# A hybrid RG-LRU, Fourier and mixture-of-experts layer on one core: the Fourier branch folded by symmetry, four gates, the gelu and one modulation moved

## The chip, the cores and the metric

One Trainium2 chip, one of its cores. The metric is the time of one execution on the device in microseconds (us), as the median of the runs. The engines are TensorE (PE; its weight loads are the rows PEld), VectorE (DVE), ScalarE (ACT), GpSimd (POOL), and SyncE (SP), which issues most DMAs.

## What is computed

384 tokens of 1024 channels: 128 context tokens and 256 latent ones, which share all weights. All matrix products are in fp32. Cut to what matters:

```python
def trunk_layer(x, mod, h0, p):
    sh1, sc1, g1, sh2, sc2, g2 = [mod[:, k, None, :] for k in range(6)]   # mod = silu(cond) @ w_ada + b_ada
    u = (x * (1.0 + sc1) + sh1) @ p['w_in']           # 1536 columns: xr, gr, xf, 512 each
    xr = centred_conv(xr, ...)
    yr, states = rglru_bidir(xr, ...)                 # gates, then one scan per direction, summed
    yr = yr * jax.nn.gelu(gr)
    yf = fourier_mix(xf, p['fn_w'], p['fn_b'])
    mix = jnp.concatenate([yr, yf], axis=-1) @ p['w_out']
    x = layer_norm(ALPHA * x + g1 * mix, ...)
    y2 = hier_moe(x * (1.0 + sc2) + sh2, ...)         # top expert group, two of its four experts of 1024x512
    return layer_norm(ALPHA * x + g2 * y2, ...), states

def fourier_mix(x, w, b):                             # 4 groups of 128 channels
    f = jnp.fft.fft2(xg, axes=(positions, channels), norm='ortho').real
    return einsum('bngi,gij->bngj', f, w) + b
```

## The kernel before, in words

The kernel is one program of five instruction streams that meet at semaphores; the order on each engine is written out by hand. Tokens lie along the free dimension for the mixer, in tiles of 388 columns (W: 128 context, 3 of padding, 256 latent, 1), and channels on the partitions.

**Weights.** SP streams 17 units of 2 MB (`p1_units`: twelve of `w_ada`, three of `w_in`, two of `w_out`) and then 48 expert units (`order`) through a ring of six, later seven, slots (L368, L387). A unit's load waits until `p1_used` or `unit_used` says that the slot's last reader is done. Expert units 3, 4 and 5 wait for `p1_used` 15, 16 and 17 (17 is the second G2 sum), unit 6 for the first LayerNorm's results.

**Modulation.** For each of twelve halves n, `ada_sums(n)` (PE, L1284, 32 columns wide) forms partial sums in a PSUM bank (ABANK), ACT copies them to the one buffer `mrow` (`ada_rows`, L446), `ada_cols(n)` (PE, L1295) turns them into columns, and DVE adds the bias (`mod_out`, L772). Halves 4 to 9 come between the mixer's branches and the output projection, 10 and 11 (second gate, G2) after it, ahead of the routing.

**Mixer.** PE computes twelve tiles of the input projection (`project(w)`, L1346: w 0 to 3 are xr, 4 to 7 xf, 8 to 11 gr) and places eight gate products among them (`gate(it)`, L1329) as GATE_WITHIN and GATE_AFTER say: 0 to 3 by tiles 4 to 6, 4 and 5 by tile 7, 6 and 7 by tile 8. ACT makes four activations of each (L480 to L488), POOL two operations (L1219, L1220), DVE two (L822, L823); after gates 3 and 7 ACT takes one square root over four gates (L491, with a table load), and DVE runs scans and sums (L828 to L848). gelu: POOL makes its argument and last product (L1229 to L1234), ACT the tanh (L495).

**Fourier branch.** For each channel group g: `chan_dft` (L1365) multiplies three token tiles by the channel DFT, 256 columns each; ACT copies the result to Z (L522, L523); `pos_dft` (L1376, L1380) multiplies by the position DFTs, two products of 128 columns and four of 256, into bank 4; DVE copies to FTs (L857); `fourier_out` (L1388) applies `fn_w` into bank 5; DVE adds the bias (L859). The groups lie one behind the other behind tiles 8 to 11, and share one bank each for result and output.

**Output projection and routing.** L1447 forms the mix in 48 products of 512 columns, with broadcasts of modulation rows between them (`row`, L1431); it begins once all of `ada_cols` to 9, `yf_sb` and `yr_done` are there. DVE makes LayerNorm and the second modulation (L904 to L917). Then PE: `ada_sums(10)`, `ada_cols(10)`, `h2_cols(0)` (eight transposes, L1460), `ada_sums(11)`, `ada_cols(11)`, `h2_cols(1)`, `logits(0)`, `logits(1)` (L1466), `h2_cols(2)`, `logits(2)`. DVE chooses the experts (L927 to L965), PE ranks the tokens (L1490, L1495), DVE builds selection matrices (L984, L994), and PE gathers each expert's tokens (`dispatch`, L1509). The sixteen experts follow (L1547, L1553, L1585, L1592, L1620), and a second LayerNorm.

## Time and profile before

| | us |
|---|---|
| median of three runs | 546.44 |
| the three runs | 542.8, 546.44, 548.4 |
| span of the profiled execution, first to last instruction | 544.4 |
| mean of the granted TensorE clock in it, as a share of full speed | 0.936 |

The profiled execution has no time of its own beside its span; the span is 2.0 us under the median of the runs. In the rows, an instruction group has its start, its duration, engine, line, operation, output<-input with shapes, and how often it occurs; in square brackets stands the engine's idle time before it and what ended that. An fp32 product is two MATMUL instructions in the rows.

### The profile page before, as it was taken

The page shows a single profiled execution, that of the slowest core. Times are in us where ns is not written, and L with a number is a line of the kernel's source. Part 1 is how long each engine was busy: PE and PEld are TensorE (multiplying, and loading weights), DVE is VectorE, ACT ScalarE, POOL GpSimd, SP SyncE. Part 2 cuts the span into 40 slices and gives each one's busy share as a digit, 9 for nine tenths or more (in the row PEclk, how much of TensorE's full clock was granted, in tenths as well). Part 3 has the DMA queues.
Part 4 walks back from the last instruction along what each step waited for, and adds up shares of the span by engine and source line. Part 5 has one row for each costly group of instructions (what it writes and reads, how often), then busy time and mean ns, then how long its engine had stood idle before and what let it go on. Part 6 is the DMA issues. An engine that isn't in the chain of part 4 may idle for free.

```text
span 544.4 us, 6675 instructions
## 1 busy us (share of the span) xinstructions
PE 465.0 (85%) x2488; PEld 261.0 (48%) x2488; DVE 244.5 (45%) x440; ACT 120.6 (22%) x224; POOL 61.4 (11%) x59
## 2 busy tenths in 40 slices
PE   0788997979899999839799999999999999899600
PEld 0444554647455653739645545455555554454200
DVE  2552626580314319565011324444444444334797
ACT  2300177841210220313401111111111111021100
POOL 1000042673400006610000000000000000000000
PEclk9989999998999999858999999999999999999855
DMA  8999692200999405950059999999999999999002
GB/s 321 387 386 291 244 390 68 96 1 18 308 389 387 169 1 184 391 198 2 1 195 389 390 392 340 396 395 393 391 393 394 395 395 393 392 391 377 11 2 116
DMA packets 64868, 146.64 MB, mean 269 GB/s; under 512 B 3560, under 2 KB 4392, under 8 KB 64824
## 3 DMA queue, kind: packets, MB, share of 16 engines
q1 hardware_dynamic: 63776, 143.66, 71.4%
q10 hardware_dynamic: 888, 2.28, 1.1%
q8 instruction: 30, 0.49, 0.4%
q0 software_dynamic: 160, 0.10, 0.3%
q14 instruction: 14, 0.11, 0.1%
HBM read 144.45 MB, written 1.58 MB: 268 GB/s over the span
## 4 chain that ended last, share of the span: by engine, by line
PE 73%; DVE 12%; DMA 5%; issue 5%; ACT 4%; ACTq 0%; SPq 0%; DVEq 0%
PE PS L1547 16%; PE PS L1346 9%; PE PS L1585 8%; PE PS L1447 8%; PE PS L1553 5%; PE PS L1284 4%; PE PS L1620 4%; DMA ring<-in_ex_w_gate 4%; PE PS L1509 4%; PE PS L1431 2%; PE PS L1295 2%; PE PS L1329 2%; PE PS L1466 2%; PE PS L1592 1%; PE PS L1627 1%
## 5 line engine op out<-in xcount | busy, mean ns | idle before, releaser
L1547 PE MATMUL PS<-ring,xs 128*64 128x256 f32 x896 | 103.1, 382 | 1.8 <-DMA ring<-in_ex_w_gate 1.1
L1547 PEld LDWEIGHTS PS<-ring,xs 128*64 128x64 f32 x896 | 62.4, 137 | 37.9 <-issue 9.7
L1346 PE MATMUL PS<-hT,ring 128*128 128x388 f32 x192 | 68.3, 510 | 3.8 <-DVE hT L793 3.8
L1585 PE MATMUL PS<-ring,hTs 128*64 128x512 f32 x224 | 52.7, 613 | 1.3 <-DMA ring<-in_ex_w_down 0.8
L1098 DVE SCALAR_TENSOR_TENSOR y<-PS,comb,y 128x1024 f32<-128x1024 f32 x42 | 53.5, 1277 | 0.3 <-PE PS L1627 0.3
L1346 PEld LDWEIGHTS PS<-hT,ring 128*128 128x128 f32 x192 | 37.8, 198 | 31.4 <-issue 5.2
L1553 PE MATMUL PS<-ring,xs 128*128 128x512 f32 x64 | 28.1, 594 | 2.9 <-ACT xs L611 2.9
L1585 PEld LDWEIGHTS PS<-ring,hTs 128*64 128x64 f32 x224 | 15.2, 140 | 31.4 <-issue 31.3
L645 ACT CAST yh<-PS 128x512 fp32r<-128x512 f32 x14 | 8.2, 586 | 97.9 <-PE PS L1585 58.1
L1084 DVE TENSOR_TENSOR yl<-PS,yh 128x512 fp32r<-128x512 f32 x14 | 9.7, 692 | 43.9 <-ACT yh L645 43.9
L1620 PE MATMUL PS<-yh,selT 64*128 64x512 f32 x84 | 21.0, 496 | 4.6 <-DVE y L1098 2.6
L1284 PE MATMUL PS<-ring,cond 128*32 128x512 f32 x192 | 23.4, 611 | 0.0
L1447 PE MATMUL PS<-ring,yfs 128*128 128x512 f32 x48 | 23.4, 633 | 0.0
L1054 DVE SCALAR_TENSOR_TENSOR hid<-sg,PS 128x256 f32<-128x256 f32 x14 | 5.9, 422 | 38.7 <-PE PS L1547 38.7
L1447 PE MATMUL PS<-ring,mixT 128*128 128x512 f32 x48 | 21.6, 592 | 0.0
L1620 PEld LDWEIGHTS PS<-yh,selT 64*128 64x128 f32 x84 | 8.0, 186 | 26.2 <-issue 26.1
L1553 PEld LDWEIGHTS PS<-ring,xs 128*128 128x128 f32 x64 | 12.0, 190 | 17.2 <-issue 17.1
L1509 PE MATMUL PS<-sel,h2H 128*128 128x384 f32 x48 | 17.9, 373 | 2.6 <-DVE sel L994 2.6
L1219 POOL TENSOR_SCALAR gtmp<-gtmp 128x388 f32<-128x388 f32 x8 | 9.5, 1188 | 85.9 <-ACT gtmp L481 85.9
L1295 PEld LDWEIGHTS PS<-cst,mrow 128*128 128x128 f32 x96 | 11.7, 191 | 13.1 <-ACT mrow L446 7.3
L446 ACT COPY mrow<-PS 128x512 f32<-128x512 f32 x12 | 7.0, 586 | 46.8 <-PE PS L1284 37.9
L1509 PE MATMUL PS<-sel,h2L 128*128 128x384 f32 x48 | 17.3, 360 | 0.0
(230 smaller groups left out, 601.3 us busy)
## 6 DMA issues: line engine op xcount, KB each, us to landing
ring<-in_ex_w_gate SPq DMA_DIRECT2D x16, 2048.0 KB, 13.8
ring<-in_ex_w_up SPq DMA_DIRECT2D x16, 2048.0 KB, 14.0
ring<-in_ex_w_down SPq DMA_DIRECT2D x16, 2048.0 KB, 14.5
ring<-in_w_ada SPq DMA_DIRECT2D x12, 2048.0 KB, 14.8
ring<-in_w_in SPq DMA_DIRECT2D x3, 2048.0 KB, 20.6
ring<-in_w_out SPq DMA_DIRECT2D x2, 2048.0 KB, 12.4
xn<-in_x_sample SPq DMA_DIRECT2D x2, 512.0 KB, 6.5
pos<-in_pos SPq DMA_DIRECT2D x2, 512.0 KB, 7.5
```

The lines of the kernel that those rows point to most:

```text
L1098: dve.scalar_tensor_tensor(out=y12[:, i, :], in0=src, scalar=comb[:, i, e:e + 1], in1=y12[:, i, :], op0=ALU.mult, op1=ALU.add).then_inc(s[ ...
L1284: mm = pe.matmul(PS[32 * j:32 * j + 32, ABANK[n], :], cond32[:, k, :], w[:, k, :], start=(k < 4), stop=(k >= 4))
L1295: mm = pe.matmul(PS[:, 7, 2 * (c0 + q):2 * (c0 + q) + 2], mrow[:, q * P:(q + 1) * P], cst[:, C_SUM:C_SUM + 2], start=True, stop=True)
L1329: mm = pe.matmul(PS[:, 4 + gi, 0:W], wbd[:, 8 * gi + 4 * d + c, :], xc[:, c, :], start=True, stop=True)
L1346: mm = pe.matmul(PS[:, w % 4, 0:W], wt[:, k, (w % 4) * P:(w % 4 + 1) * P], hT[:, k, :], start=(k == 0), stop=(k == KD - 1))
L1431: mm = pe.matmul(PS[:, 6 + k // 4, (k % 4) * P:(k % 4 + 1) * P], modT[:, j * KD + k, q:q + 1].broadcast_to([P, P]), ident, start=True, sto ...
L1447: mm = pe.matmul(PS[:, 2 * i + h, :], x, unit3(ring[(14 + h) % RING])[:, c, :], start=(n == 0), stop=(n == KD - 1))
L1509: mm = pe.matmul(PS[:, 4 + n % 4, 0:HS], part[:, i, k * P:(k + 1) * P], sel[:, i, h * HS:(h + 1) * HS], start=(i == 0 and part is h2H), st ...
L1547: mm = pe.matmul(PS[HALF * h:HALF * (h + 1), j, 0:FE // 2], x[:, k, 0:HALF], w[:, k, h * (FE // 2):(h + 1) * (FE // 2)], start=(k == 0), s ...
L1553: mm = pe.matmul(PS[:, j, :], x[:, k, :], w[:, k, :], start=(k == 0), stop=(k == KD - 1))
L1585: mm = pe.matmul(PS[HALF * h:HALF * (h + 1), 3, :], x, w[:, f, h * 512:(h + 1) * 512], start=(f == 0), stop=(f == KF - 1))
L1620: mm = pe.matmul(PS[:, b + h, :], m[HALF * h:HALF * (h + 1), i * P:(i + 1) * P], part[HALF * h:HALF * (h + 1), 0:512], start=(q == 0), sto ...
```

## The change

The Fourier branch uses symmetry and reordering. `fn_w` is multiplied into the channel DFT beforehand on chip (`chan_maps`: two products of 512 columns, copied by ACT to `maps`), and the position DFT is folded: DVE adds and subtracts mirrored positions (`folds`), so that the cosine part needs one half of the rows and the sine part the other. `chan_dft` then makes six products of 128 columns per group (two of them with 64 output rows on each half), `pos_dft` one of 128 and two of 256 columns into bank g, and its result is the output up to the bias. `FTs` and the old `fourier_out` on PE are gone. All four groups come after tile 11; `ada_sums` 4 and 5 stand between them and use banks 5 and 4.

Gates 4 to 7 move behind tiles 9, 10 and 11. The square roots become `mult(0)` (after tile 6) and `mult(1)` (after tile 11, ahead of the Z copies). The gelu's argument moves from POOL to DVE among the gates, its tanh becomes one ACT operation of 1552 columns after `ada_rows(4)`, its last product a DVE operation. `mod_out` 4 and 5 stand after two of the four gelu products. The Fourier bias is added by DVE after each scan of the second half.

After the output projection `ada_sums` 10 and 11 and `ada_cols(10)` come after `logits(2)`, `ada_cols(11)` after the ranking; ACT's and DVE's parts move with them (DVE's `mod_out` 10 and 11 behind the ranking's sums).

```diff
-        GATE_WITHIN = {5: 1, 6: 3, 7: 4, 8: 6}
-        GATE_AFTER = {4: 0, 5: 2, 7: 5, 8: 7}
+        GATE_WITHIN = {5: 1, 6: 3, 10: 5, 11: 7}
+        GATE_AFTER = {4: 0, 5: 2, 9: 4, 10: 6}
...
-        ABANK = [6, 6, 4, 6] + [6, 4] * 3 + [6, 6]
+        ABANK = [6, 6, 4, 6] + [5, 4] * 3 + [6, 6]
...
+                if w == 6:
+                    mult(0)
+                if w == 8:
+                    act.wait_ge(s["maps_ps"], 1)
+                    act.copy(maps[:, :, :], PS[:, 6:8, :]).then_inc(s["maps_sb"], 1)
+
+            def z_copy(g):
+                act.wait_ge(s["z_ps"], g + 1)
+                if g >= 2:
+                    act.wait_ge(s["f_ps"], g - 1)
+                act.copy(Z[:, g % 2, :], PS[:, 6 + g % 2, 0:TOK]).then_inc(s["z_sb"], 1)
+
+            mult(1)
+            for g in range(FG):
+                z_copy(g)
...
-            for n in range(4, 10):
+            ada_rows(4)
+            act.wait_ge(s["gelu_t"], CR)
+            act.activation(xf[:, :, :], xf[:, :, :], ACT.Tanh, scale=float(np.sqrt(2 / np.pi))).then_inc(s["gelu_th"], 1)
+            for n in range(5, 10):
                 ada_rows(n)
...
             root(NT + 1)
+            h2_copies(0)
+            h2_copies(1)
+            root(NT + 2)
+            h2_high(0)
+            h2_high(1)
+            h2_copies(2)
             ada_rows(10)
-            h2_high(0)
-            h2_copies(0)
-            root(NT + 2)
+            h2_high(2)
             ada_rows(11)
-            h2_high(1)
-            h2_copies(1)
-            h2_copies(2)
-            h2_high(2)
...
+            def folds():
+                dve.wait_ge(s["win_sb"], 8)
+                dve.wait_ge(s["conv_done"], CR)
+                dve.wait_ge(s["zeroed"], 4)
+                for n, (c0, m) in enumerate(SEG):
+                    o, h = (0, P)[n], m // 2
+                    a_, b_ = xf[:, :, c0 + 1:c0 + h], xf[:, :, c0 + m - 1:c0 + h:-1]
+                    step(dve.tensor_tensor(fold[:, :, o + 1:o + h], a_, b_, ALU.add))
+                    step(dve.tensor_tensor(fold[:, :, o + h + 1:o + m], a_, b_, ALU.subtract))
+                    step(dve.tensor_copy(fold[:, :, o:o + 1], xf[:, :, c0:c0 + 1]))
+                    step(dve.tensor_copy(nyq[:, :, n * HALF:n * HALF + 1], xf[:, :, c0 + h:c0 + h + 1]))
+                    step(dve.memset(fold[:, :, o + h:o + h + 1], 0.0))
...
+            def gelu_arg(c):
+                t_, g = xf[:, c, :], gr[:, c, :]
+                dve.wait_ge(s["win_sb"], 8 + c + 1)
+                link(dve.tensor_tensor(t_, g, g, ALU.mult))
+                link(dve.tensor_scalar(t_, t_, 0.044715, 1.0, ALU.mult, ALU.add))
+                dve.tensor_tensor(t_, t_, g, ALU.mult).then_inc(s["gelu_t"], 1)
...
             for b in range(2):
+                if b:
+                    folds()
+                    gelu_arg(0)
+                    gelu_arg(1)
...
+                    if it >= 6:
+                        gelu_arg(it - 4)
...
+                    if b:
+                        fourier_out(it - 4)
...
+            dve.wait_ge(s["gelu_th"], 1)
             for c in range(CR):
-                dve.wait_ge(s["gelu_done"], c + 1)
+                link(dve.scalar_tensor_tensor(out=gr[:, c, :], in0=xf[:, c, :], scalar=1.0, in1=gr[:, c, :],
+                                              op0=ALU.add, op1=ALU.mult))
...
+                if c == 1:
+                    mod_out(4)
+                    mod_out(5)
-            for n in range(4, 10):
+            for n in range(6, 10):
                 mod_out(n)
...
+            def chan_maps():
...
+                for h in range(2):
+                    mm = pe.matmul(PS[:, 6 + h, :], dft[:, F_CH + h * P:F_CH + (h + 1) * P],
+                                   fnw[:, :, :].rearrange("p g n -> p (g n)"), start=True, stop=True)
+                mm.then_inc(s["maps_ps"], 1)
...
             def chan_dft(g):
...
+                pe.matmul(PS[0:HALF, b, 0:P], fold[:, g, 0:HALF], co, start=True, stop=True)
+                pe.matmul(PS[HALF:P, b, 0:P], fold[:, g, HALF:P], si, start=True, stop=False)
+                pe.matmul(PS[HALF:P, b, 0:P], nyq[:, g, 0:HALF], co, start=False, stop=True)
+                pe.matmul(PS[:, b, P:2 * P], fold[:, g, P:2 * P], co, start=True, stop=True)
+                pe.matmul(PS[:, b, 2 * P:3 * P], fold[:, g, 2 * P:3 * P], si, start=True, stop=False)
+                pe.matmul(PS[:, b, 2 * P:3 * P], nyq[:, g, HALF:], co, start=False, stop=True).then_inc(s["z_ps"], 1)
 
             def pos_dft(g):
...
+                pe.matmul(PS[:, g, 0:SEQ], z[:, 0:P], dft[:, F_CTX:F_CTX + P], start=True, stop=True)
                 for m in range(2):
...
+                    mm = pe.matmul(PS[:, g, SEQ:TOK], z[:, (1 + m) * P:(2 + m) * P],
+                                   dft[:, F_LAT + LAT * m:F_LAT + LAT * (m + 1)], start=(m == 0), stop=(m == 1))
                 mm.then_inc(s["f_ps"], 1)
...
+                if w == 7:
+                    chan_maps()
+
+            pe.wait_ge(s["win_sb"], 12)
+            pe.wait_ge(s["gate_act"], 8)
+            chan_dft(0)
+            chan_dft(1)
             ada_sums(4, 7)
+            ada_sums(5, 8)
+            for g in range(FG):
+                pos_dft(g)
+                if g + 2 < FG:
+                    chan_dft(g + 2)
             ada_cols(4)
...
             pe.wait_ge(s["row_sb"], 6)
-            ada_sums(10, 15)
-            ada_cols(10)
             h2_cols(0)
-            ada_sums(11, 16)
-            ada_cols(11)
             h2_cols(1)
...
             pe.transpose(PS[0:8, 2, 128:256], stin[:, 0:8], ident).then_inc(s["st_ps"], 1)
+            ada_sums(10, 15)
+            ada_sums(11, 16)
+            ada_cols(10)
...
             mm.then_inc(s["rank_ps"], 1)
+            ada_cols(11)
```

## Rows read from the trace of the kernel before

**Rows 1.** The page's head, and the DMA engines' busy tenths in 40 slices.
```profile
span 544.4 us, 6675 instructions
DMA  8999692200999405950059999999999999999002
```

**Rows 2.** Groups by line and form on PE, 87.41 to 161.09 us: busy, mean ns, idle before.
```profile
L1284 PE MATMUL PS<-ring,cond 128*32 128x512 f32 x96 | 11.3, 597 | 0.0
L1380 PE MATMUL PS<-dft,Z 128*128 128x256 f32 x32 | 8.6, 416 | 0.0
L1365 PE MATMUL PS<-dft,xf 128*128 128x256 f32 x24 | 6.6, 415 | 0.0
L1295 PE MATMUL PS<-cst,mrow 128*128 128x2 f32 x48 | 6.3, 253 | 0.7 <-ACT mrow L446 0.7
L1329 PE MATMUL PS<-xc,wbd 128*128 128x388 f32 x16 | 5.9, 494 | 2.8 <-ACT gtmp L481 2.8
L1388 PE MATMUL PS<-FTs,fnw 128*128 128x384 f32 x8 | 3.4, 512 | 0.2 <-DVE FTs L857 0.2
L1376 PE MATMUL PS<-dft,Z 128*128 128x128 f32 x16 | 2.7, 290 | 4.6 <-DVE FTs L857 3.9 <-ACT Z L523 0.7
```

**Rows 3.** Windows: length, busy (x) of PE, PEld, DVE, ACT, POOL, then granted clock.
```profile
87.41:161.09 73.68, 65.37 (x314) 39.66 (x313) 32.47 (x60) 29.22 (x50) 30.53 (x32) 0.98 0.44 149
...
226.00:244.81 18.81, 8.90 (x60) 8.14 (x60) 8.66 (x38) 3.55 (x5) 6.08 (x5) 0.50 0.69 255
244.81:265.80 20.99, 20.94 (x108) 19.73 (x108) 8.34 (x35) 7.92 (x17) 0.00 (x0) 0.88 0.00 1
```

**Rows 4.** PE in order of time: products of known size.
```profile
103.44 1.46 PE L1365 MATMUL PS<-dft,xf 128*128 128x256 f32 x6
104.73 5.38 PE L1346 MATMUL PS<-hT,ring 128*128 128x388 f32 x16
...
166.17 3.60 PE L1447 MATMUL PS<-ring,mixT 128*128 128x512 f32 x8
...
173.04 1.95 PE L1431 MATMUL PS<-cst,modT 128*128 128x128 f32 x16
```

**Rows 5.** ACT in order of time: two gates' first activations, a table load, a square root.
```profile
92.89 0.58 ACT L480 ACTIVATE rtmp<-PS,bga 128x388 f32<-128x388 f32 x1
...
96.12 0.59 ACT L480 ACTIVATE rtmp<-PS,bga 128x388 f32<-128x388 f32 x1
...
106.62 1.28 ACT L491 ACT_TABLE_LOAD   x1
108.56 1.50 ACT L491 ACTIVATE gtmp<-gtmp 128x1552 f32<-128x1552 f32 x1 [0.65 <-DVE gtmp L823]
```

**Rows 6.** Groups by line and form on DVE, 90 to 160 us.
```profile
L848 DVE TENSOR_TENSOR xc<-hfb 128x256 f32<-128x256 f32 x4 | 2.7, 682 | 0.1
```

**Rows 7.** Groups by line and form on PE, 214.82 to 244.81 us.
```profile
L1284 PE MATMUL PS<-ring,cond 128*32 128x512 f32 x32 | 3.8, 598 | 0.0
L1295 PE MATMUL PS<-cst,mrow 128*128 128x2 f32 x16 | 2.1, 252 | 1.5 <-ACT mrow L446 1.5
```

**Rows 8.** PE in order of time, the last transposes and logits.
```profile
228.42 1.95 PE L1460 MATMUL PS<-cst,tts 128*128 128x128 f32 x8
231.47 3.61 PE L1466 MATMUL PS<-wr,h2T 128*128 128x20 f32 x16 [1.10 <-ACT h2T L547]
```

**Rows 9.** DVE in order of time: the last h2, the routing's first and last steps.
```profile
221.55 1.28 DVE L914 SCALAR_TENSOR_TENSOR tts<-tts,stat,rows 128x1024 f32<-128x1024 f32 x1
...
235.11 0.22 DVE L927 TENSOR_TENSOR lg<-PS,rb 128x60 f32<-128x60 f32 x1 [9.14 <-PE PS L1466]
...
241.12 0.21 DVE L965 TENSOR_TENSOR before<-rt 128x48 bf16<-128x48 f32 x1
```

**Rows 10.** The chain that ended last, in order of time: start, us, what.
```profile
161.09 12.10 PE PS L1447 x24
...
451.47 19.65 DMA ring<-in_ex_w_gate
```

More of the change, by code:

```diff
@@ L216, in build @@
         xf = at("xf", o, [P, FG, W]); o += FG * W * 4
-        Z = at("Z", o, [P, 2, NT, 2 * P]); o += 2 * NT * 2 * P * 4
+        Z = at("Z", o, [P, 2, TOK]); o += 2 * TOK * 4
         dft = at("dft", o, [P, NDFT]); o += NDFT * 4
+        maps = at("maps", o, [P, 2, FG * P]); o += 2 * FG * P * 4
         fnw = at("fnw", o, [P, FG, P]); o += FG * P * 4
         hfb = at("hfb", o, [P, 2, W]); o += 2 * W * 4
+        nyq = at("nyq", o, [P, FG, HALF + P]); o += FG * (HALF + P) * 4
         assert o <= end
@@ L488, in gate, with mult @@
                 act.activation(tr, a_, ACT.Square).then_inc(s["sq_done"], 1)
-                if q == 3:
-                    act.wait_ge(s["rec_v"], it + 1)
-                    act.activation(gtmp[:, 2], gtmp[:, 2], ACT.Sqrt, scale=-1.0).then_inc(s["mult_done"], 1)
-            def gelu_tanh(c):
-                act.wait_ge(s["gelu_t"], c + 1)
-                act.activation(xpad[:, c, 0:W], xpad[:, c, 0:W], ACT.Tanh, scale=float(np.sqrt(2 / np.pi)))\
-                    .then_inc(s["gelu_th"], 1)
+            def mult(b):
+                act.wait_ge(s["rec_v"], 4 * b + 4)
+                act.activation(gtmp[:, 2], gtmp[:, 2], ACT.Sqrt, scale=-1.0).then_inc(s["mult_done"], 1)
             for w in range(12):
@@ L516, in _ @@
                     gate(GATE_AFTER[w])
-                if w >= 8:
-                    act.wait_ge(s["z_ps"], c + 1)
-                    if c >= 2:
-                        act.wait_ge(s["f_ps"], c - 1)
-                    act.copy(Z[:, c % 2, 0:2, :], PS[:, 6, :].rearrange("p (i n) -> p i n", n=256))
-                    act.copy(Z[:, c % 2, 2, :], PS[:, 7, 0:256]).then_inc(s["z_sb"], 1)
-                    gelu_tanh(c)
+                if w == 6:
[11 more added lines that the diff above has]
+                z_copy(g)
             for r, n in enumerate(("ln_in_g", "ln_in_b")):
@@ L918, in _ @@
                     .then_inc(s["x1n"], 1)
-            for n in range(10, 12):
-                mod_out(n)
             low_part(0)
@@ L978, in _ @@
             dve.nop().then_inc(s["pw_done"], 1)
+            for n in range(10, 12):
+                mod_out(n)
             def pick(m):
@@ L1353, in chan_dft @@
             def chan_dft(g):
-                pe.wait_ge(s["win_sb"], 4 + g + 1)
                 if g == 0:
-                    pe.wait_ge(s["smallw_in"], 32)
-                    pe.wait_ge(s["mod_sb"], 4)
-                    pe.wait_ge(s["mrow_sb"], 4)
-                else:
-                    pe.wait_ge(s["z_sb"], g)
-                for i in range(NT):
-                    out = PS[:, 6, i * 256:(i + 1) * 256] if i < 2 else PS[:, 7, 0:256]
-                    mm = pe.matmul(out, xf[:, g, TC[i]:TC[i] + P], dft[:, F_CH:F_CH + 256], start=True, stop=True)
@@ L1366, in chan_dft @@
-                mm.then_inc(s["z_ps"], 1)
+                    pe.wait_ge(s["maps_sb"], 1)
+                    pe.wait_ge(s["fold_done"], 1)
+                if g >= 2:
+                    pe.wait_ge(s["z_sb"], g - 1)
+                b = 6 + g % 2
+                co, si = (maps[:, h, g * P:(g + 1) * P] for h in range(2))
+                pe.matmul(PS[0:HALF, b, 0:P], fold[:, g, 0:HALF], co, start=True, stop=True)
+                pe.matmul(PS[HALF:P, b, 0:P], fold[:, g, HALF:P], si, start=True, stop=False)
```

72 lines of the change are left out of this document (19 added, 53 removed).

## The prediction, made before the changed kernel was run

> **What bounds the kernel now.** I read the page first: a span of 544.4 us, 2.0 under the median of the runs, and a DMA row that is at 9 from slice 20 to slice 36 [rows 1], so the experts' weights stream without a pause from about 275 us on. The chain of waits then puts PE at nearly every step up to there, and only late, at 451.47 us, a piece of 19.65 us on an expert load [rows 10]. The stream of expert units beyond the seven that are preloaded starts when the first expert product ends. Whether PE or the stream ends last among the experts, both hang on the moment at which the experts start. So what is won or lost ahead of them passes to the end one for one, and I take the experts and the final LayerNorm as unchanged.
>
> Ahead of them are two stretches in which PE isn't filled. From 87.41 us (gate 4) to 161.09 us (start of the output projection) PE is busy 65.37 of 73.68 us [rows 3], so it idles 8.3 us. The groups name 8.3 of it: 2.8 ahead of the gates, 4.6 and 0.2 in the Fourier branch, 0.7 ahead of the last `ada_cols` [rows 2]. From the end of the projection, which I call E (214.82 us), to the dispatch at 244.81 us [rows 3], PE works through small products and then waits for DVE's routing; the clock is at the low level, 0.50, from 226.00 us on and stays there for some 5 us of dispatch (0.88 over 20.99 us is 5.0 us at half) [rows 3].
>
> **Stretch 1, what goes.** The old Fourier products are L1380, L1365, L1388 and L1376: 8.6 + 6.6 + 3.4 + 2.7 = 21.3 us [rows 2]. A printed group runs about 0.17 us into its successor (1.46 us, but the next starts after 1.29 [rows 4]); for 16 such groups that is 2.7, so 18.6 us of PE's time go.
>
> **What comes.** `chan_maps`: two products of 512 columns. Eight instructions of that size take 3.60 - 0.17 = 3.43 us [rows 4], 0.43 each, so four take 1.7. `chan_dft`: six products of 128 columns, twelve instructions; sixteen take 1.78 [rows 4], 0.111 each, so 1.33 per group and 5.3 for four. The trace before has no fp32 product with 64 output rows at this size. If the two halves ran side by side a group would take 1.1, and if each product cost as much as one of 256 columns (0.43) it would take 2.6: 4.4 to 10.4 us, and I take 5.3, as 128 columns are the row nearest. `pos_dft`: 0.22 + 2 x 0.43 = 1.08, four are 4.3. Sum 11.3. PE's work falls by 18.6 - 11.3 = 7.3 us.
>
> A rule of the Trainium skill speaks against the new `chan_dft`: TensorEngine Tiling (Array Packing), Key Properties, says that a change between tiling modes drains TensorE. The L1284 products are 32 wide and alternate with 128-wide ones, and their groups have 0.0 us of idle before them over 96 instructions [rows 2]; by the rule eight more switches would cost something, by the row nothing that can be seen, and I take nothing.
>
> **Laying out the new order on PE.** After gate 3 there is no Fourier work and no gate until tile 9. From 87.4 us: 4.5 tiles at 5.21 (16 instructions, 5.38 - 0.17 [rows 4]) are 23.4, four gates (5.9 - 4 x 0.17) 5.2, the maps 1.7: tile 11 ends at about 117.7. ACT needs 3.23 us per gate with a copy (96.12 - 92.89 [rows 5]) where PE gives it one each 3.9, so it keeps up: gate 4 from 103.6, with a table load of 1.28 [rows 5], gate 7 done at 118.1, last copy 118.6. `chan_dft` 0 and 1: to 121.4. Sums 4 and 5 are 2 x 1.8 (11.3 us for six, less overlaps [rows 2]): to 125.0. They cover `mult(1)`: DVE's last reciprocal parts end at 119.5, table load and square root (1.28 + 1.50 [rows 5]) at 121.4, the Z copies by 122.4. This cover is 2.6 us; without it PE would wait that long. The rest of the Fourier work, 7.0: to 132. Then four sums (7.2) and six `ada_cols` (6.3 less overlaps, 5.9), with 1.4 us of waits for ACT: the tanh over 1552 columns (by the square root 1.50, plus a load of 1.28) stands ahead of `ada_rows(5)` and costs 0.5 of it. The projection starts at 146.6 instead of 161.09, 14.5 earlier. The other account, 7.3 of work and 8.3 - 2.3 of idle, gives 13.3. I take 14.0.
>
> Beside the path: `folds` handles 1520 elements per partition and six tiny ones. At 682 ns for 256 [rows 6] that is 4.0 us, at half that rate 2.0; it lies between DVE's last scan of the first half (about 97.5) and gate 4's results (107.9), with `gelu_arg(0)`, as tile 9's copy (102.7) holds `gelu_arg(1)` back anyway. Its cover is about 5 us; beyond that it delays gates 6 and 7 by the recurrence's waits, one for one. Three gelu operations of 388 elements are at most 3.1 us per tile by the same row, hidden while ACT paces DVE. DVE's Fourier bias waits for `f_ps` between scans, where the next scan is queued behind it; this ends by 134.5. The tanh ends at 134.5, four times 1.45 us of products end at 140.3, and the projection asks for them first at 146.6: 6 us of cover. `mod_out` 4 and 5, which `ada_cols(6)` waits for, come at 137.4, just in time. POOL loses 20 operations, none on the path. On SP's queue the loads of `w_out` wait for sums 4 and 5, which move from 143 and 148 to 123 and 125 us, 20 us before use. No stall here.
>
> **Stretch 2.** The two sums and `ada_cols` pairs leave PE's path ahead of the transposes: L1284 with 3.8 us, L1295 with 2.1 and 1.5 of waits [rows 7]. `h2_cols(0)`, `(1)` and `logits(0)`, `(1)` then end by about E + 6. What is late next is DVE's third h2, ready at 222.83, E + 8.0 [rows 9]; `h2_cols(2)` ran at 228.42, E + 13.6 [rows 8]. It moves 5.6 us ahead. From there to DVE's first routing step are 6.7 us at the low clock [rows 8, 9]; I keep them, since only transposes and products of 20 columns then stand between E and the logits, and the clock fell before in just such work. Logits at E + 14.7. DVE's selection takes 6.2 (235.11 to 241.33 [rows 9]): E + 20.9. PE's moved work must fit beneath it: the state's transpose 0.4, sum 10 at the low clock 3.8 (2 x 1.9 [rows 7]), ACT's copy 0.6, sum 11. Dispatch brought the clock back after 5 us of dense work; by that it is back at E + 20.2, sum 11 ends at E + 21.8, `ada_cols(10)` at E + 22.8: ranking starts 1.9 late. From there to the dispatch 3.5 as before (241.33 to 244.81), plus 0.3 for the two `mod_out` that now stand ahead of the selection matrices: E + 26.6 instead of E + 30.0, a gain of 3.4. Dispatch begins at the full clock: 2.5 of its 5 slow us were not spent waiting for DVE's matrices, and half of that is 1.2. Sum 4.6.
>
> Expert units 4 to 6 wait behind the moved sums: unit 6 is loaded by about E + 40 at 5.3 us each and is read some 90 us after E. Nothing waits.
>
> **Sum.** 14.0 + 4.6 = 18.6 us: span 525.8, and on the median 546.4 - 18.6 = **527.8 us**.
>
> **The rivals.**
> *The clock is full through the routing.* The last logits end at E + 11.9, the sums lie beneath the selection (E + 18.1), dispatch at E + 21.9: 8.1 + 1.2, 23.3 in all: 523.1 us. For it: sums are dense and now come late. Against: the 11 us behind E are thinner than before.
> *The clock stays low until dispatch.* Then sum 11 ends at E + 23.3, `ada_cols(10)` at E + 25.3, and `ada_cols(11)` takes 2.0 ahead of DVE's `mod_out`: dispatch at E + 29.9, no gain in stretch 2, 14.1 in all: 532.3 us. For it: the low level held through 226.00 to 244.81 [rows 3]. The Trainium skill, TensorE: Matmul & The Clock Gate, Part 4, says that transposes do not count as PE being busy, which makes an earlier fall likely; the trace agrees in so far as the fall came among transposes and logits.
> *The tail of the second gates bounds PE.* The idle of 8.3 us stays, now as waits for Z, tanh or `mod_out`: 12.6 in all, 533.8 us. For it: `mod_out` has no slack and ACT has a table load on each side. Against: sums 4 and 5 fill the largest gap.
> *Slower: the folds.* Reversed rows of a three-dimensional tile are in no row before. From 5 us on they delay the gates; from 5 + 18.6 = 23.6 us on (15.5 ns per element, six times the row) the kernel is slower. At 30 us it would be 552.8.
> *Nothing arrives*, because the experts' end does not follow their start: 546. Against: [rows 1].
>
> **How the numbers follow.** Forecast 0.42, full clock 0.17, low clock 0.21, tail 0.14, folds 0.03, nothing 0.03. One per cent is about what a measurement of this kernel can tell from no change. Faster by over 1% (under 541) 0.94, within 1% 0.03, slower 0.03. The runs before lie 3.6 below to 2.0 above their median; I take the full clock less 3 as the low end, the tail plus 3 as the high end: 520 to 537, which leaves out some 0.15 with what scatters. The dear `chan_dft` (5.1 more) ends at 532.9, inside.
>
> **What would show it.** In the profile after: tile 11 ends near 118 us, the first L1447 product near 147, and PE's idle from gate 4 on is 2 to 3 us; the new `chan_dft` takes 1.3 us a group; the folds 2 to 4 us in all. The third transposes start 8.0 us after E, DVE's routing at E + 14.7, dispatch at E + 26.6; the clock is low from about E + 5 to E + 20. The experts take as long as before from dispatch to end. It is wrong if a wait over 2 us stands ahead of `pos_dft`, `ada_cols` or the first mix product, or if experts wait longer for weights.

## The result, and the profile after

The changed kernel takes 531.41 us, median of 4 runs (530.14 to 532.37), beside 547.42 us (542.8 to 551.39, 4 runs) for the kernel before on the same chip: 16.0 us less. The run of 551.39, 1.6% above the fastest, counts as a slow one: without it the kernel before has 546.44 and the gain is 15.0 us, and the ratio, 0.9739 with the interval 0.9691 to 0.9787, goes by fast runs alone. The forecast was 527.8 (520 to 537). The profiled execution has a span of 528.9 us, 15.5 under the span of before [rows 1], where the sum had promised 18.6. So the question is less whether there is a gain than where the missing 3 us went.

I cut both kernels at the same moments, read from PE in order of time, so that each stretch has a length of its own. E is taken here less the 0.17 that a group runs into its successor, 214.65 for the kernel before where the prediction says 214.82.

```
                                      before    after   change   forecast
start to the first projection           31.07    33.36    +2.3      0
first projection to gate 3              49.82    49.57    -0.25     0
gate 3 to the first mix product         80.07    66.06   -14.0    -14.0
first mix product to E                  53.69    53.70     0        0
E to the dispatch                       30.16    25.59    -4.6     -3.4
dispatch, first to last product         20.95    21.48    +0.5     -1.2
last dispatch to first expert product    2.92     2.93     0        0
first expert product to the end        275.72   276.21    +0.5      0
span                                   544.4    528.9    -15.5    -18.6
```

**Stretch 1** (gate 3 to the first mix product) came out to a tenth. PE's groups by line and form, kernel after, 92.06 (the maps) to 148.99 us (first mix product), beside [rows 2]:

```profile
L1315 PE MATMUL PS<-ring,cond 128*32 128x512 f32 x96 | 11.3, 597 | 0.0
L1326 PE MATMUL PS<-cst,mrow 128*128 128x2 f32 x48 | 6.2, 252 | 1.0 <-ACT mrow L448 1.0
L1360 PE MATMUL PS<-xc,wbd 128*128 128x388 f32 x16 | 5.9, 489 | 0.0
...
L1403 PE MATMUL PS<-maps,fold 128*64 128x128 f32 x8 | 1.7, 298 | 0.8 <-ACT gr L512 0.8
```

The waits of 2.8 ahead of the gates and of 4.6 and 0.2 in the Fourier branch [rows 2] are gone; left are 1.0 for ACT's row copies and 0.8 for its copy `gr`. The windows from gate 3 on give the split. A row has the length, then PE's, PEld's, DVE's, ACT's and POOL's busy time, then the granted clock:

```profile
80.89:160.96 80.07, 71.76 (x334) 43.33 (x332) 35.15 (x64) 34.53 (x58) 33.78 (x36) 0.98 0.42 142
```

is the kernel before, and

```profile
82.93:148.99 66.06, 64.20 (x330) 37.63 (x328) 39.32 (x86) 33.51 (x51) 15.26 (x16) 1.00 0.54 184
```

is the kernel after. PE's busy time falls by 71.76 - 64.20 = 7.6 and its idle from 8.3 to 1.9, by 6.4. Not all of the 7.6 is work that went. In the kernel before, a wait for DVE's `FTs` was followed by the low level of the clock (PE in order of time):

```profile
122.42 0.68 PE L1376 MATMUL PS<-dft,Z 128*128 128x128 f32 x4 [2.61 <-DVE FTs L857]
122.94 2.90 PE L1380 MATMUL PS<-dft,Z 128*128 128x256 f32 x8
125.63 2.18 PE L1365 MATMUL PS<-dft,xf 128*128 128x256 f32 x6
```

The same two groups take 1.89 and 1.46 elsewhere (133.95 and 135.68), so 1.7 us of the old busy time came from the clock. The stretch's granted clock was 0.98 before and is 1.00 now. For the kernel after, PE in order of time shows what a channel group of the new `chan_dft` costs:

```profile
120.82 0.32 PE L1403 MATMUL PS<-maps,fold 128*64 128x128 f32 x1 [0.81 <-ACT gr L512]
120.82 0.32 PE L1404 MATMUL PS<-maps,fold 128*64 128x128 f32 x1
...
121.95 0.39 PE L1408 MATMUL PS<-maps,nyq 128*128 128x128 f32 x2
122.27 0.32 PE L1403 MATMUL PS<-maps,fold 128*64 128x128 f32 x1
...
123.72 3.64 PE L1315 MATMUL PS<-ring,cond 128*32 128x512 f32 x32
127.29 0.49 PE L1414 MATMUL PS<-dft,Z 128*128 128x128 f32 x2
127.62 1.03 PE L1416 MATMUL PS<-dft,Z 128*128 128x256 f32 x4
...
129.71 0.39 PE L1408 MATMUL PS<-maps,nyq 128*128 128x128 f32 x2
129.94 0.39 PE L1414 MATMUL PS<-dft,Z 128*128 128x128 f32 x2
```

From one group to the next are 122.27 - 120.82 = 1.45 us (forecast 1.33). The two halves with 64 output rows start at the same moment. The Trainium skill, TensorEngine Tiling (Array Packing), Key Properties, says that tiles can run in parallel, and the trace agrees. With the halves side by side the forecast's own prices give 1.1 for a group, so the measured 1.45 is 0.35 above them, and not only 0.12. Part of that lies where the width changes: L1408 takes 0.32 us up to the next product where that is 64 wide (121.95 to 122.27), and 0.23 where it is 128 wide (129.71 to 129.94). `ada_cols` shows the same 0.09, with 1.05 behind a 32-wide sum (140.62, no wait) and 0.96 behind a 128-wide product (134.65). The same section says that a change of mode drains TensorE; the trace agrees in so far as each change goes with some 0.1 us, which stands inside the busy time and not in the idle column. A group has two changes; the rest of the 0.35 stays open.

Sums 4 and 5 cover the square root of `mult(1)` in full: no wait stands at 127.29. On DVE the reversed fold of 508 elements per partition costs 1.34 ns per element, half of what I had taken:

```profile
99.72 0.68 DVE L833 TENSOR_TENSOR fold<-xf 128x508 f32<-128x508 f32 x1
...
102.32 0.56 DVE L847 TENSOR_TENSOR xf<-xf,gr 128x388 f32<-128x388 f32 x1
```

The second row, a product that reads forwards, costs 1.44 ns per element, so reading backwards costs nothing that can be seen here. The row that I had priced by, L848, is a poor measure: its eight instructions before took 280 to 941 ns, for a reason that stays open.

The whole of `folds` is 2.4 us, from 98.90 to 101.3 (forecast 4.0, low bound 2.0).

**Stretch 2** (E to the end of the dispatch), PE in order of time, kernel after. E is 202.69:

```profile
204.92 4.87 PE L1495 MATMUL PS<-wr,h2T 128*128 128x20 f32 x32 [0.32 <-ACT h2T L555]
210.87 1.97 PE L1489 MATMUL PS<-cst,tts 128*128 128x128 f32 x8 [1.08 <-DVE tts L955]
213.94 3.60 PE L1495 MATMUL PS<-wr,h2T 128*128 128x20 f32 x16 [1.10 <-ACT h2T L555]
...
217.68 3.50 PE L1315 MATMUL PS<-ring,cond 128*32 128x512 f32 x16
221.99 1.92 PE L1315 MATMUL PS<-ring,cond 128*32 128x512 f32 x16 [0.81 <-ACT mrow L448]
...
228.28 0.66 PE L1538 MATMUL PS<-sel,h2H 128*128 128x384 f32 x1 [1.61 <-DVE sel L1035]
```

The same products have two prices by the clock's level: a sum of 16 products takes 3.50 at 217.68 and 1.92 at 221.99. So the clock fell within the first logits, about E + 5, and was back by E + 19.3, much as forecast. What I had not foreseen is that it fell again in the wait of 1.61 behind the thin ranking (granted 1.00 up to 227.50, 0.64 from there to 228.28): the dispatch begins with products of 0.66 that take 0.33 later. The granted clock of the dispatch was 0.88 over 20.99 us before [rows 3]; now it is 0.85:

```profile
228.28:249.76 21.48, 21.48 (x108) 20.26 (x108) 8.33 (x35) 7.91 (x16) 0.00 (x0) 0.85 0.53 196
```

That is 21.48 x 0.15 x 2 = 6.4 us at the low level instead of 5.0.

The mix, too, starts at the low level, in both kernels. In the kernel after:

```profile
148.07 1.05 PE L1326 MATMUL PS<-cst,mrow 128*128 128x2 f32 x8 [0.73 <-ACT mrow L448]
148.99 5.38 PE L1476 MATMUL PS<-ring,yfs 128*128 128x512 f32 x8
```

Eight such products take 3.60 later, so 1.8 us are lost here; the granted clock was 1.00 up to 148.99 and 0.50 from 150 to 152. The kernel before has the same 5.38 at 160.96, so the change neither causes nor cures it.

**The opening**, which the change doesn't touch. PE in order of time, first before, then after:

```profile
20.07 2.49 PE L1284 MATMUL PS<-ring,cond 128*32 128x512 f32 x16
...
25.45 1.92 PE L1284 MATMUL PS<-ring,cond 128*32 128x512 f32 x16
```

```profile
19.85 3.43 PE L1315 MATMUL PS<-ring,cond 128*32 128x512 f32 x16
...
26.16 3.52 PE L1315 MATMUL PS<-ring,cond 128*32 128x512 f32 x16
```

The first two sums are the same instructions on the same data, and cost 2.5 us more. Whether this belongs to the change was the first thing to test.

### The profile page after: what moved, and what is told of

It is laid out like the page before. It is cut to its first block, busy times and chain, and to the rows that moved or that the text cites. A ratio compares the mean times of both kernels' runs of the same rounds, so it can differ in the third digit from the quotient of the medians.

```text
span 528.9 us, 6658 instructions
## 1 busy us (share of the span) xinstructions
PE 461.6 (87%) x2484; PEld 255.8 (48%) x2484; DVE 250.6 (47%) x462; ACT 119.5 (23%) x218; POOL 43.0 (8%) x40
## 4 chain that ended last, share of the span: by engine, by line
PE 79%; DVE 9%; DMA 5%; ACT 3%; issue 2%; ACTq 1%; DVEq 0%; SPq 0%
PE PS L1576 17%; PE PS L1377 12%; PE PS L1614 8%; PE PS L1476 8%; PE PS L1582 5%; PE PS L1315 5%; PE PS L1649 4%; PE PS L1538 4%; DMA ring<-in_ex_w_gate 4%; PE PS L1621 3%; PE PS L1460 2%; PE PS L1360 2%; PE PS L1326 2%; PE PS L1656 1%; DMA rowB<-in_colsB 1%
## 5 line engine op out<-in xcount | busy, mean ns | idle before, releaser
L1315 PE MATMUL PS<-ring,cond 128*32 128x512 f32 x192 | 27.6, 703 | 0.8 <-ACT mrow L448 0.8
L1649 PEld LDWEIGHTS PS<-yh,selT 64*128 64x128 f32 x84 | 7.8, 183 | 26.6 <-issue 26.5
L1083 DVE SCALAR_TENSOR_TENSOR sg<-sg,PS 128x256 f32<-128x256 f32 x14 | 5.9, 421 | 24.8 <-ACT sg L628 24.8
## 6 DMA issues: line engine op xcount, KB each, us to landing
ring<-in_ex_w_down SPq DMA_DIRECT2D x16, 2048.0 KB, 14.5
```

The source lines that it names most:

```text
L1315: mm = pe.matmul(PS[32 * j:32 * j + 32, ABANK[n], :], cond32[:, k, :], w[:, k, :], start=(k < 4), stop=(k >= 4))
L1649: mm = pe.matmul(PS[:, b + h, :], m[HALF * h:HALF * (h + 1), i * P:(i + 1) * P], part[HALF * h:HALF * (h + 1), 0:512], start=(q == 0), sto ...
```

## Experiments

All kernels below are complete: none leaves out or changes part of the computation, and three of them add products that nobody reads. The table has the median and range of each with its ratio to the kernel before, then, from its profiled execution, the start of the first projection, gate 3 to the first mix product, E to the dispatch, E to the dispatch's end, first expert product to the end, and the span.

```
kernel          median  range          ratio [interval]          proj   mix    disp   d.end  rest    span
before_again    549.39  543.8-552.4    1.0027 [0.9980, 1.0074]   33.10  80.23  30.57  51.13  278.04  548.3
after_again     532.02  531.6-532.9    0.9721 [0.9634, 0.9808]   33.61  66.06  25.61  47.07  276.70  529.6
a_only          533.77  532.4-535.6    0.9759 [0.9670, 0.9849]   31.80  66.05  30.13  51.13  276.56  530.2
b_only          543.94  540.6-545.3    0.9927 [0.9885, 0.9969]   32.39  80.09  25.47  46.86  275.78  539.7
gates_old       533.26  531.6-536.3    0.9744 [0.9664, 0.9823]   31.24  69.05  25.74  47.58  277.70  532.0
gelu_pool       532.25  530.5-533.2    0.9711 [0.9640, 0.9782]   32.24  66.09  25.74  47.61  277.45  530.9
mod_late        538.14  534.9-540.3    0.9810 [0.9729, 0.9891]   31.85  73.42  25.74  47.30  279.18  538.2
mod_late_fill   532.25  530.4-534.8    0.9711 [0.9635, 0.9786]   32.28  68.63  25.62  47.07  276.14  529.8
g2_between      529.48  527.5-532.0    0.9683 [0.9588, 0.9778]   31.35  66.05  25.05  45.66  276.20  525.7
g2_fill         526.96  526.6-528.5    0.9618 [0.9551, 0.9686]   30.98  66.05  26.03  46.00  275.03  524.5
g2_fill_open    524.25  523.5-525.4    0.9566 [0.9500, 0.9633]   30.09  66.05  24.74  44.37  276.15  521.3
```

**Both kernels again.** No edit.

> The changed kernel as it is, beside the runs of the parts. In its first profile the opening (two `ada_sums` at the low clock, 3.41 and 3.47 us instead of 2.47 and 1.90 before) had cost 2.1 us ahead of anything that the change touches. Theory: that is scatter of the clock, so in this profile the first product of the input projection starts anywhere from 31 to 34 us, and from there on the times repeat: last tile before the maps to first mix product 56.9 us, mix end to dispatch 25.6. Rival: the opening belongs to the change, and starts at 33.4 again.

> The kernel before, for a second profile of it. Its runs spread from 543 to 552 us, its first profile was at 544.4. Theory: the spread is the clock at the opening and behind the mix; from gate 4 (87.41 us then) to the first mix product it takes 73.6 us again and from the mix's end to the dispatch's end 50.9, and what is longer lies ahead of gate 4. Rival: the Fourier tail itself varies, through the low clock in it, and that stretch is over 1 us off.

From gate 3 to the dispatch's end the stretches repeat to 0.2 us in both kernels (66.06 twice, 80.07 and 80.23), except that before's dispatch begins 0.4 later. The experts repeat less well: before's take 278.04 instead of 275.72, and 1.7 of that is the first expert product, which takes 15.69 instead of 13.99 although nothing was changed. The opening doesn't repeat either. The kernel before, run again, has it at 33.10:

```profile
19.67 3.25 PE L1284 MATMUL PS<-ring,cond 128*32 128x512 f32 x16
...
25.81 3.59 PE L1284 MATMUL PS<-ring,cond 128*32 128x512 f32 x16
```

Over the kernels that leave the opening alone it lies between 30.98 and 33.61. So the 2.3 us are scatter of the clock in code that is the same, and the profile before had drawn a good opening. The second pair of profiles differs by 18.7 us (548.3 and 529.6), the first by 15.5; that 18.7 is so close to the forecast's 18.6 is luck, as the experts' scatter is in it. More runs of before give medians of 547.4 to 549.4 where the first three gave 546.4; that this is the opening is likely in part and not shown, since of the 3.9 us between its two profiles 2.0 lie in the opening and 2.3 behind the dispatch.

**One part at a time.** `a_only` keeps the mixer's part and puts stretch 2 back; `b_only` moves the second gate's sums in the kernel before. The diff is `a_only`'s on PE against the changed kernel; ACT's and DVE's orders go back likewise, and `b_only` is the same lines the other way on the kernel before.

```diff
+            ada_sums(10, 15)
+            ada_cols(10)
             h2_cols(0)
+            ada_sums(11, 16)
+            ada_cols(11)
             h2_cols(1)
...
-            ada_sums(10, 15)
-            ada_sums(11, 16)
-            ada_cols(10)
...
-            ada_cols(11)
```

> The mixer's part alone (folded Fourier branch, moved gates, gelu on VectorE); the second gate's sums stay ahead of the transposes as before. Theory: the two parts add. Gain over the kernel before 12 to 14.5 us (ratio 0.974 to 0.978), with the stretch from the mix's end to the dispatch again near 30 us. Rival: the parts share a cause, as the clock after the mix, and this part alone is within 2 us of the whole change.

> The second gate's sums inside the routing alone, on the kernel before. Theory: gain 3.5 to 4.6 us (ratio 0.992 to 0.994), mix end to dispatch 25.6 to 26.6 us instead of 30.0, third transposes 8.1 us after the mix's end. Rival: the clock stays low until the dispatch and the gain is under 1 us.

The parts add up stretch by stretch: `a_only` has 66.05 and 51.13, `b_only` 80.09 and 46.86, the changed kernel 66.06 and 47.07. Neither disturbs the other. By the ratios of the table, all taken beside the same runs of before, the mixer's part is worth 2.4% and the routing's part 0.7%, and both together 2.8%; the intervals are 0.8 to 1.8% wide, so the stretches show the sum better than the ratios do.

**The gates' places.** The Fourier branch stays folded, but gates 4 to 7 stand at their old tiles, the folds and `mult(1)` stand where the old gates need them, and the gelu's argument and the Fourier bias come after DVE's scans.

```diff
-        GATE_WITHIN = {5: 1, 6: 3, 10: 5, 11: 7}
-        GATE_AFTER = {4: 0, 5: 2, 9: 4, 10: 6}
+        GATE_WITHIN = {5: 1, 6: 3, 7: 4, 8: 6}
+        GATE_AFTER = {4: 0, 5: 2, 7: 5, 8: 7}
```

> The changed kernel with gates 4 to 7 back by tiles 7 and 8 (second square root behind tile 8, folds and gelu arguments moved to fit). Theory: what the moved gates bring is PE's wait of 2.8 us ahead of gate 5, since the folded branch behind all tiles removes the other waits in either order. The wait of 2.8 us returns ahead of gate 5; the Z copies no longer stand behind the square root, but PE's two sums cover that anyway: the stretch from the third quarter of tile 7 to the first mix product grows from 59.5 to 62 us, 2 to 3 us slower than the changed kernel. Rival (the moved gates are what carries the gain, as they take ACT out of the Fourier tail): the stretch grows by more than 5 us.

The stretch is 69.05, 3.0 longer, and one wait is all of it:

```profile
94.65 1.54 PE L1358 MATMUL PS<-xc,wbd 128*128 128x388 f32 x4 [2.99 <-ACT gtmp L483]
```

This is the wait of 2.8 ahead of the gates [rows 2], which the later places remove. Of the 14.0 us 3.0 are thus the gates' places and 11.0 the rest: less work, its order behind the sums, and the 1.7 us of low clock that stood behind one of the old waits.

**The gelu's argument on POOL.** The three operations per block go from DVE to POOL, behind its last item and a wait for `fold_done`.

> The changed kernel with the gelu's argument back on GpSimd, behind its eight gate items, all else the same. Theory: the arguments are done near 131 us (119 plus four times 2.9), the tanh asks for them at 135.8, so nothing moves: within 0.5 us of the changed kernel in the stretch from the maps to the first mix product (56.9). Rival (VectorE's place among the gates is what makes the tanh early enough): the tanh and with it the fifth `ada_cols` come later and that stretch grows by over 1 us.

66.09 us: no difference. POOL has the last argument ready at 133.7 us, DVE had it at 123.3, and ACT begins the tanh at 135.97 here and 135.76 there, behind its own earlier work. The move to VectorE brings nothing by itself.

**How much slack `mod_out` has.** In the changed kernel DVE's `mod_out(4)` and `(5)`, two instructions of 0.24 us together from 140.09 on, end 0.3 us before `ada_cols(6)` starts at 140.62. Here they come after all four gelu products:

```diff
-                if c == 1:
-                    mod_out(4)
-                    mod_out(5)
-            for n in range(6, 10):
+            for n in range(4, 10):
                 mod_out(n)
```

> The changed kernel with VectorE's `mod_out` 4 and 5 behind all four gelu products instead of behind two. Theory: the sixth `ada_cols` needs them and starts at 140.6 in the changed kernel, VectorE would make them at 143.3: PE waits 2.3 to 2.8 us there, and the mix starts that much later. Rival: other slack in the chain of sums, copies and columns takes it up and it is under 1 us.

The stretch grew by 7.4 us (66.05 to 73.42), where the theory had 2.3 to 2.8 and the rival under 1. PE in order of time:

```profile
137.50 1.92 PE L1312 MATMUL PS<-ring,cond 128*32 128x512 f32 x16
141.87 1.77 PE L1323 MATMUL PS<-cst,mrow 128*128 128x2 f32 x8 [2.45 <-DVE modT L780]
143.57 3.64 PE L1312 MATMUL PS<-ring,cond 128*32 128x512 f32 x16
147.14 1.87 PE L1323 MATMUL PS<-cst,mrow 128*128 128x2 f32 x8
148.94 3.54 PE L1312 MATMUL PS<-ring,cond 128*32 128x512 f32 x16
```

The wait is 2.45, as expected. But the sums behind it take 3.64 and 3.54 instead of 1.92, and `ada_cols` 1.77 and 1.87 instead of 1.05: 3.3 + 1.5 = 4.8, and 2.45 + 4.8 = 7.3. So the theory that formed was: the wait drops the clock, and the drop costs twice the wait; the rival is that something else in the moved steps slows PE. To tell them apart, the wait stays, and PE forms three products of 512 columns in it whose result nobody reads:

```diff
+                if n == 6:
+                    pe.wait_ge(s["iota_in"], 16)
+                    for _ in range(3):
+                        pe.matmul(PS[:, 6, :], ident, cst[:, C_IOTA:C_IOTA + 512], start=True, stop=True)
                 ada_cols(n)
```

> The kernel with `mod_out` 4 and 5 behind all gelu products, and three dummy products of 512 columns on TensorE in the wait of 2.45 us ahead of the sixth `ada_cols` that this made (their result is not read). Theory: that wait cost 7.4 us and not 2.4, because the clock fell to the low level behind it for some 10 us; with dense work in its place the clock holds, and the stretch from gate 3 to the first mix product is 68.5 to 69 us instead of 73.4 (66.05 in the changed kernel). Rival: the sums and columns of 32 and 2 columns were slow for another reason than the idle time, and the stretch stays over 72 us.

```profile
140.72 2.84 PE L1449 MATMUL PS<-cst 128*128 128x512 f32 x6
143.40 0.95 PE L1323 MATMUL PS<-cst,mrow 128*128 128x2 f32 x8
144.28 1.92 PE L1312 MATMUL PS<-ring,cond 128*32 128x512 f32 x16
...
151.66 3.68 PE L1477 MATMUL PS<-ring,yfs 128*128 128x512 f32 x8
```

68.63 us: the products fill the gap, the length of the delay stays (+2.6), and the 4.8 behind it is gone. The mix, too, starts at the full level (3.68 for its first eight products, 5.19 to 5.38 in all other kernels), and is 1.7 shorter, so that from gate 3 to E only 0.9 of the delay are left. The median falls from 538.14 to 532.25. The clock is shown to be the cause of the 4.8; the rival falls. How three products at 140.72 bring the full level to the mix at 151.66, behind the same wait of 0.73, stays open. The changed kernel with its own `mod_out` and such products was not run.

**Stretch 2, dense work among the logits.** Sum 10 stands ahead of the first logits and sum 11 ahead of the last transposes, with ACT's row copies in step.

```diff
             h2_cols(1)
+            ada_sums(10, 15)
             pe.wait_ge(s["rtr_in"], 64)
             logits(0)
             logits(1)
+            ada_sums(11, 16)
             h2_cols(2)
...
-            ada_sums(10, 15)
-            ada_sums(11, 16)
             ada_cols(10)
```

> The changed kernel with the second gate's first sum between the second transposes and the first logits, and the second sum ahead of the third transposes, where PE waited 1.08 us for VectorE. Theory (the thin work behind the mix lets the clock fall, dense sums hold it): the clock stays at the full level up to the last logits, which come 12 to 13 us after the mix's end instead of 14.9, and the dispatch at 22 to 23 instead of 25.6: 2.5 to 3.5 us faster than the changed kernel. Rival (sums of 32 columns don't hold the clock, as transposes and logits don't): the clock falls as before, the third transposes come about 1 us later, the gain of the shorter tail is given back, and the time is within 1 us of the changed kernel.

```profile
202.76 1.92 PE L1315 MATMUL PS<-ring,cond 128*32 128x512 f32 x16
204.62 3.75 PE L1495 MATMUL PS<-wr,h2T 128*128 128x20 f32 x32
208.30 1.92 PE L1315 MATMUL PS<-ring,cond 128*32 128x512 f32 x16
...
212.34 2.79 PE L1495 MATMUL PS<-wr,h2T 128*128 128x20 f32 x16 [1.10 <-ACT h2T L555]
...
221.96 0.17 PE L1518 MATMUL PS<-marks,tri_ones 128*128 128x16 bf16 x1 [5.11 <-DVE before L1004]
```

The 32 logit products take 3.75 here and 4.87 in the changed kernel. Over all profiles they take 3.75 in the three that have a sum between transposes and logits, and 3.93 to 5.19 in the ten that have none: with the sum between, the full level lasts through them. The Trainium skill, TensorE: Matmul & The Clock Gate, Part 4, says that transposes don't count as PE being busy in the same way; that alone doesn't decide here, as the same 16 transposes stand ahead in both kernels.

The price is that PE is empty for 5.11 us while DVE selects, and the dispatch begins at the low level. It starts at E + 25.05, where the theory had 22 to 23, and ends 1.4 earlier, at E + 45.66. So the clock was held as the theory said, and the gain was not: neither account is right as a whole. The first expert product takes 15.69 us instead of 13.99, but it does so in `before_again` too, so this edit need not be the cause. The spans of this kernel and of `after_again` differ by 3.9, of which 2.3 are the opening (31.35 and 33.61); the medians differ by 2.5.

**Filling PE's waits in stretch 2.** On top of that, unread products of 512 columns: one ahead of the last logits, five ahead of the ranking, two ahead of the dispatch, three ahead of the experts.

```diff
+            def dense(n):
+                for _ in range(n):
+                    pe.matmul(PS[:, 3, :], ident, cst[:, C_IOTA:C_IOTA + 512], start=True, stop=True)
```

> The kernel with the second gate's sums between transposes and logits, with dummy products of 512 columns (not read) in TensorE's waits: one ahead of the last logits, five ahead of the ranking, two ahead of the dispatch, three between dispatch and first expert. Theory: the low clock behind the mix is what idle and thin work bring; held at the full level the last logits take 1.8 us instead of 2.8, dispatch runs at the full clock from its start, the first expert product takes 13.99 us instead of 15.69: dispatch's end at 43.5 to 44.5 us after the mix's end instead of 45.66, first expert at 46.5 to 47.5 instead of 48.58, 3 to 5 us faster than the changed kernel in the profile from the mix's end on. Rival: the dummy products find the clock low already, take twice their time and stand in the way: no earlier than 45.66.

```profile
214.70 4.54 PE L1488 MATMUL PS<-cst 128*128 128x512 f32 x10
221.88 0.17 PE L1525 MATMUL PS<-marks,tri_ones 128*128 128x16 bf16 x1 [2.65 <-DVE before L1004]
...
223.81 3.76 PE L1488 MATMUL PS<-cst 128*128 128x512 f32 x4
226.58 1.31 PE L1546 MATMUL PS<-sel,h2H 128*128 128x384 f32 x1
```

Five products don't fill the wait: 2.65 us are left and the clock falls. The two products ahead of the dispatch then cost 3.76 us at the low level and delay it, to E + 26.03. Half a remedy, and the rival's outcome: the dispatch's end (46.00) is no better than `g2_between`'s, where the theory had 43.5 to 44.5. The first expert product takes 13.99 with the wait ahead of it cut from 2.92 to 0.35.

**The opening, too.** Short unread products ahead of the first transposes, `ada_cols` and projection, as the experiment on the opening's scatter.

```diff
+            def early(n, b=7):
+                for _ in range(n):
+                    pe.matmul(PS[:, b, 256:256 + C_IOTA], ident, cst[:, 0:C_IOTA], start=True, stop=True)
...
+                early((8, 3, 0)[i])
```

> The kernel before this one in the list (dummy products in the routing) with further small dummy products of 202 columns in TensorE's waits of the opening: eight ahead of the first transposes, three ahead of the second, one ahead of each of the first two `ada_cols`, three ahead of the first input projection. Theory: the opening's scatter (first projection at 31.1 to 33.6 us) is the clock, which thin work lets fall at one or another moment; with the waits filled both first sums take 1.9 us and the projection starts near 30 us, each run within 1 us of the others. Rival: the clock stays low at the start whatever is done, the fillers take twice their time, and the projection starts at 33 us or later.

```profile
11.02 4.82 PE L1334 MATMUL PS<-cst 128*128 128x202 f32 x16 [2.22 <-DVE cond L745]
...
19.66 1.92 PE L1315 MATMUL PS<-ring,cond 128*32 128x512 f32 x16
...
24.47 1.92 PE L1315 MATMUL PS<-ring,cond 128*32 128x512 f32 x16
...
219.26 0.17 PE L1534 MATMUL PS<-marks,tri_ones 128*128 128x16 bf16 x1 [1.07 <-DVE before L1004]
...
222.60 0.41 PE L1555 MATMUL PS<-sel,h2H 128*128 128x384 f32 x1
```

Both early sums take 1.92 and the first projection starts at 30.09, earlier than in any other kernel. Gate 3 starts at 78.11, in the kernels without these products at 79.84 to 83.17. The routing is that of `g2_fill`, but the clock fell elsewhere: sum 11 took 3.06 us, partly at the low level, PE reached its five products 1.6 us later after E, and only 1.07 us of wait were left ahead of the ranking. From there on the clock holds, and the whole dispatch has it full:

```profile
222.60:242.23 19.63, 18.96 (x110) 18.10 (x110) 8.32 (x35) 7.70 (x16) 0.00 (x0) 1.00 0.01 3
```

This rests on where the clock fell in this one execution; in `g2_fill`, with the same routing, 2.65 us of wait were left and the dispatch began at the low level.

524.25 us, a ratio of 0.9566 (0.9500 to 0.9633): it beats the kernel before and the changed kernel. Its four runs lie within 1.9 us (the theory had 1), but those of `g2_fill` do too, and those of the changed kernel lie within 2.2. So the range doesn't show that the opening holds in every run; one profile shows it.

## Why the forecast was right, and where it was off

- **What bounds the kernel: right.** What is won ahead of the experts passes to the end. (The nines of the DMA row [rows 1] begin at slice 21, counted from 0, and not at 20, which changes nothing.) From the first expert product to the end all kernels take 275.0 to 279.2 us; the changed kernel's 0.5 over before is inside that, and its source stays open. A good part of the scatter is the first expert product: where it took 13.99 us the rest is 275.0 to 276.7, where it took 15.4 to 16.9 it is 276.2 to 279.2.
- **Stretch 1, 14.0: right in sum, partly by terms that make up for each other.** The 14.0 was chosen between two accounts, 14.5 and 13.3. The busy time falls by 7.6 (forecast 7.3) and idle by 6.4 (8.3 - 2.3 = 6.0). But 1.7 of the busy time was the low clock behind the wait of 2.61; it stood in the rows that the prediction priced as work, and went with the wait without having been reasoned about. Shifted by the 2.0 that gate 3 is late in this profile, tile 11 ends at 118.0 (forecast 117.7) and the first mix product starts at 147.0 (146.6, or with the 14.0 taken 147.1). The new products were dearer than forecast: the four `chan_dft` took 5.6 (5.3) and the four `pos_dft` 4.6 (4.3), 1.08 each only where no change of width lies beside them; the maps' 1.71 was right. That the change of width costs nothing was read from the idle column, where its 0.1 us doesn't appear; that the two halves run side by side, which the sum didn't take, hid most of it. The folds were priced 1.6 too high, off the path.
- **Cover for `mod_out`: right and narrower than it reads.** "Just in time" was 0.3 us. By the way the prediction prices waits, its loss would cost its own length; `mod_late` shows three times that, 7.4 us for a wait of 2.45.
- **Stretch 2, dispatch at E + 26.6: 1.2 too late.** By the prediction's E, 0.17 later than the table's, the third transposes start at E + 8.0 and the routing at E + 14.7, both as forecast, and the clock fell and came back where it should. The ranking starts at E + 21.9 instead of 22.8, since sum 11 and `ada_cols(10)` were quicker, and the dispatch follows 3.5 behind it instead of 3.8: E + 25.4.
- **"Dispatch begins at the full clock": wrong.** Written as a gain of 1.2, it was a loss of 0.5. The step took the level at E + 20 to last until E + 26.6, across the ranking's products of 16 columns and the wait behind them; in that wait, of 1.61, it fell. The size was right: where the dispatch did have the full clock throughout, in `g2_fill_open`, it took 19.63, 1.3 less than before. The term is 1.7 short; with the 1.2 of the last point the stretch gave 4.04 instead of 4.6.
- **What the sum left out: the opening.** I took unchanged code to take unchanged time. Its two sums cost 1.92 to 3.64 us each by the level of the clock, and the profile before lay at the low end, so profile against profile loses 2.0 us that the change has no part in. Sum: 14.0 + 4.04 - 2.04 - 0.5 = 15.5.
- **The rivals.** The full clock through the routing (523.1) was not this kernel's case. Its mechanism is real in part: with the waits filled the dispatch ends at E + 44.37 instead of 47.07, but it begins at E + 24.74, not at the rival's 21.9. The low clock until dispatch is refuted by sum 11's 1.92; the tail as bound by an idle of 1.9 us; the folds by 2.4 us; that nothing arrives by the shift of the experts' start.

## What to carry to other kernels

Price a wait on TensorE by what stands behind it, not by its own length: dense work after a wait of 2.45 us cost another 4.8. Rows of a stretch at the low level hold that price too: what looks like work to be saved may be the clock. When work is moved to fill one gap, look at the next thin place, since the level at the first dense product sets its price. And compare stretches, not spans: unchanged code moved by 2 to 3 us from one execution to the next, more than half of what the smaller of the two edits was worth.

## What was not expected of the hardware

- A wait of 2.45 us drew 4.8 us of slow products behind it, and three unread products in the gap took those 4.8 away (73.42 to 68.63, in medians 538.14 to 532.25). Waits of 0.31 ahead of `ada_cols(5)` and 0.81 between the sums 10 and 11 left the level where it was, as did one of 1.07 ahead of the ranking where one of 2.65 in its place was followed by the low level. Length alone doesn't decide: one of 0.73 between two thin `ada_cols` was followed by the low level at the mix in twelve of the thirteen profiles.
- The first two sums scatter between 1.92 and 3.64 us in identical code, and a row of unread products ahead of them set both to 1.92 in the one execution profiled.
- A product next to a change between 128-wide and narrower products took some 0.1 us longer (0.32 against 0.23 us, 1.05 against 0.96), inside the busy time.
- VectorE read a row of a three-dimensional tile backwards at 1.34 ns per element (0.68 us for 508), no dearer than a product that reads forwards at 1.44 (0.56 us for 388).
